# A two-block transformer kernel on Trainium2: the late modulation tiles of the first block are issued from GpSimd's queue instead of SyncE's

## The reference

```python
def hybrid_layer(x, c, positions, w_mod, b_mod, g_pre, g_post, w_in, w_out, ...):
    mod = jax.nn.silu(c) @ w_mod + b_mod
    shift, scale, gate = jnp.split(mod, 3, axis=-1)
    h = rms_norm(x, g_pre) * (1.0 + scale[:, None, :]) + shift[:, None, :]
    proj = h @ w_in
    # sliding-window attention, spatial gating and gated linear attention
    # on parts of proj; y is their concatenation times silu(z)
    out = y @ w_out
    return x + gate[:, None, :] * rms_norm(out, g_post)

def first_block(x, c, ...):
    for l in range(DEPTH):                       # DEPTH = 2
        x = hybrid_layer(x, c, positions, w_mod[l], ...)
    return x
```

## Time and profile before

| | |
|---|---|
| median of 3 runs | 2957.92 us |
| lowest, highest | 2957.55, 2958.32 us |
| span of the profiled execution, first to last instruction | 2956.5 us |
| mean granted TensorE clock | 0.978 |
| TensorE (PE) busy | 2812.9 us, 95% |
| VectorE (DVE) busy | 1795.8 us, 61% |
| ScalarE (ACT) busy | 1375.4 us, 47% |
| GpSimd (POOL) busy | 38.6 us, 1% |
| SyncE's queue (q1) | 583.08 MB, 59.1% of the 16 DMA engines' time |
| GpSimd's queue (q0) | 19.98 MB, 2.2% |

### The profile page before, as it was taken

The page is one execution under the profiler, slowest core; times in us unless marked ns, Lnnn a source line. Parts: engine busy times, 40 slices in busy tenths (PEclk is TensorE's granted clock), DMA queues, the critical chain, the costliest instruction groups (busy, mean ns, idle before and its releaser), DMA issues.

```text
span 2956.5 us, 35707 instructions
## 1 busy us (share of the span) xinstructions
PE 2812.9 (95%) x13336; PEld 2325.3 (79%) x13336; DVE 1795.8 (61%) x2196; ACT 1375.4 (47%) x1780; POOL 38.6 (1%) x69
## 2 busy tenths in 40 slices
PE   5799977699999999999999999999999999999998
PEld 4577855588887788888888888878888888888886
DVE  6878767777874655555455445575655544545565
ACT  4355532455554444444455544444444445445443
POOL 0000010000000000000000000000000000000000
PEclk8899988899999999999999999999999999999999
DMA  9975488686565555556555555655554655555664
GB/s 392 357 271 192 164 267 289 242 281 219 173 214 170 190 171 172 177 198 201 192 171 171 179 185 191 223 168 174 178 178 160 226 193 177 172 178 174 197 212 149
DMA packets 160232, 605.16 MB, mean 205 GB/s; under 512 B 18441, under 2 KB 18593, under 8 KB 154577
## 3 DMA queue, kind: packets, MB, share of 16 engines
q1 hardware_dynamic: 155376, 583.08, 59.1%
q0 software_dynamic: 4704, 19.98, 2.2%
HBM read 600.85 MB, written 2.14 MB: 204 GB/s over the span
## 4 chain that ended last, share of the span: by engine, by line
PE 67%; DVE 1%; ACT 0%; issue 0%; DVEq 0%; ACTq 0%
PE acc L780 62%; PE psT L728 1%; PE psS L761 1%; PE psS L751 1%; PE psT L734 1%; PE psS L768 0%; DVE x L487 0%; PE psT L724 0%; DVE x L486 0%; DVE x L468 0%; DVE x L470 0%; DVE stats L453 0%; DVE xlo L440 0%; DVE x L446 0%; ACT xhi L322 0%
## 5 line engine op out<-in xcount | busy, mean ns | idle before, releaser
L434 DVE TENSOR_TENSOR wlo<-raw,whi 128x1024 fp32r<-128x1024 f32 x672 | 822.8, 1225 | 865.3 <-ACT whi L317 863.8
L317 ACT ACTIVATE whi<-raw 128x1024 fp32r<-128x1024 f32 x672 | 711.4, 1059 | 995.1 <-PE acc L780 984.8
L780 PE MATMUL acc<-whi,xhi 128*128 128x512 f32 x2304 | 638.0, 398 | 2.5 <-DVE xlo L440 1.5
L780 PE MATMUL acc<-whi,xlo 128*128 128x512 f32 x2304 | 619.5, 390 | 0.0
L780 PE MATMUL acc<-wlo,xhi 128*128 128x512 f32 x2304 | 619.4, 390 | 0.0
L780 PEld LDWEIGHTS acc<-whi,xlo 128*128 128x128 f32 x2304 | 433.1, 188 | 92.5
L780 PEld LDWEIGHTS acc<-wlo,xhi 128*128 128x128 f32 x2304 | 433.0, 188 | 91.6
L780 PEld LDWEIGHTS acc<-whi,xhi 128*128 128x128 f32 x2304 | 423.0, 188 | 83.5 <-DVE xlo L440 3.5
L1386 ACT ACTIVATE whi<-raw 128x1024 fp32r<-128x1024 f32 x240 | 253.6, 1058 | 445.8 <-PE acc L2128 250.3
L1605 DVE TENSOR_TENSOR wlo<-raw,whi 128x1024 fp32r<-128x1024 f32 x240 | 291.6, 1222 | 114.1 <-ACT whi L1386 113.2
L2128 PE MATMUL acc<-whi,hhi 128*128 128x512 f32 x864 | 255.0, 418 | 41.2 <-DVE hlo L1616 41.1
(11 more groups left out here) (313 smaller groups left out, 1925.7 us busy)
## 6 DMA issues: line engine op xcount, KB each, us to landing
raw<-in_w SPq DMA_DIRECT2D x912, 512.0 KB, 3.5
mraw<-in_w_mod SPq DMA_DIRECT2D x128, 512.0 KB, 5.0
b_y<-in_w_mod SPq DMA_DIRECT2D x12, 1024.0 KB, 10.8
mraw<-in_w_mod SPq DMA_DIRECT2D x7, 1024.0 KB, 10.0
scr<-in_w_mod SPq DMA_DIRECT2D x7, 1024.0 KB, 11.7
sgl<-in_w_mod SPq DMA_DIRECT2D x6, 1024.0 KB, 13.4
gate_row<-in_bg POOLq DMA_DIRECT2D x16, 256.0 KB, 4.9
gb<-cum_rows POOLq DMA_DIRECT2D x2, 1536.0 KB, 8.8
```

What stands on the lines that cost most here:

```text
L317: act.activation(whi[:, n % SLOTS, :], raw[:, n % SLOTS, :], ACT.Copy).then_inc(s_hi, 1)
L434: dve.tensor_tensor(wlo[:, n % SLOTS, :], raw[:, n % SLOTS, :], whi[:, n % SLOTS, :].bitcast(F32), ALU.subtract).then_inc(s_lo, 1)
L780: m = pe.matmul(acc[c % 2][:, tb, :], a[:, kk, tb * P:(tb + 1) * P], b[:, n % SLOTS, k * CW:(k + 1) * CW], start=(kk == 0 and q == 0), sto ...
```

## The change

`half` moves, unchanged but for the engine, from SyncE's program to GpSimd's. It still waits for the same count of `s_macc`, loads the same 512 KB into the same half of `mraw` and raises the same semaphore. SyncE's loop keeps the weights alone. GpSimd's loop over layers is written out: the parameters of layer 0; tiles 0 to 33; the gate rows of layer 0 (`gate_rows(0)`); tiles 34 and 35; the read back into `gain` (`gains(0)`); tiles 36 to 95; the parameters of layer 1; tiles 96 to 127; gate rows and gain of layer 1. (`GATED` is [31, 127], the last tile of each gate; `SCALED[-1]` is 95, the last tile of layer 1's shift and scale.) VectorE's order, with `LATE_AT`, stays as it is.

```diff
--- before.py
+++ after.py
@@ -1295,13 +1295,6 @@
             kt, third = n // 2, 1 - n % 2
             sp.dma_start(big[n % len(big)], dram["w_mod"][0, third, kt]).then_inc(s_m[n % len(big)], 16)
 
-        def half(i):
-
-            l, third, kt, part = LATE[i]
-            sp.wait_ge(s_macc, late_free(i))
-            sp.dma_start(mraw[:, i % 2, :], dram["w_mod"][l, third, kt, :, part * MOD_W:(part + 1) * MOD_W])\
-                .then_inc(s_m[len(big) + i % 2], 16)
-
         def weights(n):
             if n >= SLOTS:
                 sp.wait_ge(*split(n - SLOTS))
@@ -1321,11 +1314,8 @@
                 tile(n)
             for n in range(4 * j + 4, 4 * j + 8):
                 weights(n)
-        for n in range(4 * GPC + 4, DEPTH * GRAN1 + 2):
-            if n < DEPTH * GRAN1:
-                weights(n)
-            for i in LATE_AT.get(divmod(n - 2, GRAN1), []):
-                half(i)
+        for n in range(4 * GPC + 4, DEPTH * GRAN1):
+            weights(n)
         for n in range(SLOTS if s_next else 0):
             sp.wait_ge(*split(DEPTH * GRAN1 - SLOTS + n))
             sp.dma_start(raw[:, n, :], dram["w"][n]).then_inc(s_next[n], 16)
@@ -1363,19 +1353,40 @@
             pool.affine_select(out=sgw, in_=sgw, compare_op=ALU.is_ge, fill=0.0, base=0,
                                pattern=[[0, S_G], [1, P]], channel_multiplier=-1).then_inc(s_sgw, 1)
 
-        parameters(0)
-        for l in range(DEPTH):
+        def half(i):
+
+            l, third, kt, part = LATE[i]
+            pool.wait_ge(s_macc, late_free(i))
+            pool.dma_start(mraw[:, i % 2, :], dram["w_mod"][l, third, kt, :, part * MOD_W:(part + 1) * MOD_W])\
+                .then_inc(s_m[len(big) + i % 2], 16)
+
+        def gate_rows(l):
 
             pool.wait_ge(s_gcol, l + 1)
             need(pool, (s_gain, 16 * l))
             pool.dma_start(dram["gate"].rearrange("(k p) -> p k", p=P), gcol[:],
                            allow_slow_non_contiguous=True).then_inc(s_gbuf, 16)
+
+        def gains(l):
             pool.wait_ge(s_gbuf, 16 * (l + 1))
             pool.wait_ge(*filled(("go", l, 1)))
             pool.wait_ge(s_gx, len(LEVELS) * (l + 1))
             pool.dma_start(gain[:], dram["gate"].partition_broadcast(P)).then_inc(s_gain, 16)
-            if l + 1 < DEPTH:
-                parameters(l + 1)
+
+        parameters(0)
+        for i in range(GATED[0] + 3):
+            half(i)
+        gate_rows(0)
+        for i in range(GATED[0] + 3, GATED[0] + 5):
+            half(i)
+        gains(0)
+        for i in range(GATED[0] + 5, SCALED[-1] + 1):
+            half(i)
+        parameters(1)
+        for i in range(SCALED[-1] + 1, GATED[1] + 1):
+            half(i)
+        gate_rows(1)
+        gains(1)
 
     @block.scalar
     def _(act):
```

## The result

The changed kernel takes 2975.74 us (median of 4 runs, 2972.43 to 2977.74) against 2958.12 us for the kernel before on the same chip (4 runs, 2957.55 to 2959.96): ratio 1.0056, 95% interval 1.0043 to 1.0068. It is slower by 17.6 us. The prediction was slower, 2969 us within 2950 to 2990. The profiled span grows from 2956.5 to 2976.0 us.

A forecast was written before the change was run, and what follows sets the result against it. The closed round trip of tiles through two buffers was taken to set the pace up to 541 us, TensorE later. +14 us for 50 tiles and -3 for the parameters gave +11, 2969 us, range 2950 to 2990.

The forecast's parts named there:

- the prediction's own formula: Whole kernel: time is 2957.9 + 25 x (0.27 + D) - 3 us, D being the change of a tile's landing.
- rival two: Closed-loop tiles: landing stays between 4.0 and 4.5 us, total between -5.9 and +5.9 us; at 4.4, 2962 us; chance 0.22.
- The 50 tiles of the sum: Closed loop, 8 tiles in steps 82 to 87 and 42 from step 93 to the layer's end: +14 us.
- The parameters' term of -3: Second layer's parameters, moved from 412 us to behind tile 95, give back 3 us over some 7 tiles.
- rivals one and three: Same 50 tiles: one, freed queue, landing 3.9 us, 2949 us, chance 0.18; three, descriptors wait for VectorE, 3000 us, chance 0.07.
- rival four: Both queues equal in every way, only the parameters' place differs: 2955 us; counted inside rival two, no chance of its own.
- The wake-up, +0.27 us per turn: Buffer turn: GpSimd issues a tile 0.30 us after VectorE's end, SyncE 0.03 us; not hidden, +0.27 us per turn.
- The landing, D = +0.3: Closed-loop tiles: a tile's time from issue to landing grows by 0.3 us on GpSimd's queue, from 4.4 us.
- The first 26 tiles: 0, at most 2: First 26 tiles: VectorE's own work and a full TensorE beside them, so loss 0, at most 2 us.
- layer 1: 0, at most +4: 16 tiles from 560.1 to 607.6 us: loop nearly closed, but TensorE busy 47.73 of 48 us; 0, at most +4 us.
- The gate rows: Tiles 34 and 35 queue behind the gate rows on GpSimd: from 2 less to 4 more us, taken as 0.
- ScalarE's wait for weights nearly gone: Steps 97 to 119: ScalarE's wait for weights nearly vanishes while VectorE's wait for tiles grows.

The follow-up runs named there:

- the relay: Changed kernel, but GpSimd only signals and SyncE issues the tiles between the weights, with a larger clearing (128x384) for a 0.57 us lag: 2960.51 us, ratio 1.0009.
- the relay kernels: Two versions of the changed kernel where GpSimd signals and SyncE issues tiles and weights: 2956.00 us (lag 0.19 us) and 2960.51 us (lag 0.57 us).
- the late parameters alone: Kernel before, with only the second layer's parameters held back to where the change puts them, all tiles on SyncE's queue: 2955.41 us, ratio 0.9987.

## Why the prediction was right, and where its steps failed

**Sign and size** came out: +11 forecast, +17.6 measured, inside the range. The closeness is partly luck. By the prediction's own formula the landing that was measured, 4.4 us (D = 0), gives 2957.9 + 25 x 0.27 - 3 = 2962 us, which is rival two, "the same". The 50 tiles of the sum lost 10 us where 14 were forecast, and 13 us came from places that it had put at nothing: the start, the first tiles and the second layer. The parameters' term of -3 stands (-3.8 by the ratio). Right too were the place of the loss up to 541 us, the 0.30 us wake-up, the pace (3.26 us a tile, 3.3 forecast), VectorE's wait, and the far side of 608 us; rivals one and three are out (median landing 4.4 us, no lost 1.23 us), and so is rival four, 2955 us. (The range did not take in "most of rival one": its 2949 us lies just below 2950.)

**The wake-up, +0.27 us per turn**, held in the changed kernel: of the 0.33 us by which the round trip grew, 0.26 are lag, and 0.38 us more lag lengthened the loop by 6.1 us where half a turn each gives 6.8. What failed is the reason given for it, that a lag inside the turn can't be hidden. In one queue it was: the relay's 0.57 us left 106.3 us against 106.8. I had read the 3.05 us pace as a closed chain, which it is, and missed that the transfer inside the chain shrinks or stretches with what else is queued. Over the whole kernel 0.27 us is worth 3 us beside one queue and 8 beside two, with 6.75 forecast.

**The landing, D = +0.3**, is the term that failed. The median landing stayed at 4.4 us, the mean rose by 0.05 to 0.2. What grew is the sum of lag and landing, 4.7 to 5.0 us, by 0.3 on the mean of five profiles, and that is the lag, which a landing in one queue would have given back. The hope that a tile no longer queues behind weights didn't come true either: it was the weights that landed 1.0 us sooner. In the loop 35 x 0.33 / 2 = 6 of the 7.4 us follow from it (114.2 less 106.8); forecast was 36 x 0.57 / 2 = 10.

**"The first 26 tiles: 0, at most 2"** and **"layer 1: 0, at most +4"** were mis-sized: +3.2 us over tiles 0 to 20 and +7.4 over 80 to 95 (for these, six profiles in one queue have a mean of 49.8 us and six in two queues 55.4, so that 5.6 is the fairer number). The cover I named, a TensorE busy 47.73 of 48 us, was not deep enough: it was full because the tiles came just in time, and the longest landing went from 5.7 to 7.6 us between the kernels that differ in this stretch's queue. The span's growth adds up from the table: 3.2 (tiles 0 to 20), 2.8 (24 to 33, forecast 2.3 for its 8 tiles), -2.5 (33 to 44, with the parameters' -3), 7.4 (44 to 79, forecast 10), 7.4 (80 to 95), -1.0 behind tile 95, and 2.2 that the first tile already started later, which the second profile doesn't show (-0.3): 19.5 us. **The gate rows** stayed at nothing: 14.0 us from their issue to the gain's became 15.7, yet tile 34 starts 14.2 us after tile 33, 14.4 before. (It stands at 403.7 us, not near 396, by the 8 us lost ahead of it.)

**"ScalarE's wait for weights nearly gone"** was wrong: 95.6 us. The slots of the weights are freed by work that is itself behind the tiles, and the 1.0 us by which they land sooner doesn't outweigh that; with SyncE's waits put back the time was the same.

On the mechanism: the Trainium skill, DMA: Bandwidth & Descriptors (Queues, rings and completion order), says that each DMA engine takes turns between the queues that have work, a packet at a time. The runs fit that and don't prove it: with two queues the weights, issued behind a tile, landed in 4.8 us instead of 5.8, and a tile's landing no longer shortened when it was issued later. The same page (Rules for kernel authors) advises that spreading DMAs over several issuing engines doesn't help bandwidth and only saves issue time; here it cost 17 us.

What is shown: most of the loss needs the tiles apart from the weights and a loop of two buffers; GpSimd's wake-up alone doesn't make it, nor the parameters, nor the early issue of the weights. What stays open is which part of "apart" does it: the second queue, the weights no longer being held behind the tile, or the time that GpSimd takes to make its own transfers ready. In the first layer it rests on the relay kernels, which change all three together (and the lag, 0.19 against 0.30 us, worth 1 to 3 us).

## What to carry to other kernels

In a loop with two buffers, ask for the whole round trip and where its transfer queues, not for the issue's latency alone: a lag in front of a queue that tiles and weights share was mostly given back here, the lag in front of a second queue was not. A stage whose engine is full only because its data comes just in time is no cover. And if a closed loop sets the pace, look for another buffer first: two freed halves of a tile were worth 34 us over the late parameters alone (0.9872 against 0.9987), where the choice of the queue was worth 20.

## What the hardware showed that I had not expected

- A lag of 0.53 us more on each of 128 issues cost 6.5 us with one queue; 0.38 us more cost 12 us with two. (Both with some 4 to 6 us to either side.)
- A tile that GpSimd signals and SyncE issues starts 0.19 us after VectorE's end, sooner than the 0.30 us of GpSimd's own issue; its small clearing took 0.10 us of that.
- With four buffers the traffic of tiles and weights ran at 360 to 378 GB/s with the DMA engines busy 0.97 to 0.98, against 266 GB/s and 0.78 in the changed kernel: the two-buffer loop, not the DMA, had been the limit.
